# Gate and forget-logit projection of the forgetting branch: moved into the stick-breaking attention, one tile per step

## The reference

```
proj = h @ w_in
(q_r,k_r,v_r,g_r, q_s,k_s,v_s,g_s, q_f,k_f,v_f,g_f, f_logit) = split(proj)
o_r = group_norm(retention(rotary(q_r), rotary(k_r)/8, v_r))          # 6 heads of 64
o_s = stick_breaking(q_s, [cached k, k_s], [cached v, v_s])           # 5 heads
logf = log_sigmoid(f_logit + b_f);  C = cumsum(logf)                  # 5 heads
o_f = softmax(rms(q_f) . [cached k, rms(k_f)] / 8 + C_t - C_s) @ v    # 5 heads, causal
x = x + concat(o_r*silu(g_r), o_s*silu(g_s), o_f*silu(g_f)) @ w_out
x = x + (p @ w_pe) * sigmoid(rms_norm(x) @ w_pg)
```

## Time and profile before

| what | us |
|---|---|
| median of three runs | 3673.13 (3656.63 to 3677.41) |
| profiled execution: its own time | 3678.38 |
| profiled execution: span from first to last instruction | 3676.8 |
| TensorE, matmuls | 3204.2 busy (87%) |
| TensorE, weight loads | 1989.8 busy (54%) |
| VectorE | 1365.4 busy (37%) |
| ScalarE | 950.5 busy (26%) |
| GpSimd | 597.8 busy (16%) |
| mean granted TensorE clock | 0.929 of full |

### The profile page before, as it was taken

One profiled execution on the slowest core, in us unless ns is written; L12 is line 12 of the kernel. 1 busy time (PEld: TensorE's weight loads), 2 busy tenths in 40 slices (PEclk: granted clock), 3 DMA queues, 4 the chain that ended last, 5 costly groups with the idle time before them and its releaser, 6 DMA issues. The chain is left out here.

```text
span 3676.8 us, 67694 instructions
## 1 busy us (share of the span) xinstructions
PE 3204.2 (87%) x25256; PEld 1989.8 (54%) x25256; DVE 1365.4 (37%) x3002; ACT 950.5 (26%) x1746; POOL 597.8 (16%) x1090
## 2 busy tenths in 40 slices
PE   6999987888998688799989998978889987887998
PEld 4556654555666455444455666545556654554443
DVE  3235086443224444312142350954433244442211
ACT  2012144332224333211020122433322242331110
POOL 0000000444010044400000000004440101452000
PEclk9999988999999799899989999989999997998999
DMA  5011103887120388710120011048861205995102
GB/s 175 18 36 33 50 10 105 265 287 244 38 83 1 117 278 290 249 66 16 46 96 28 28 45 44 1 129 288 284 217 33 72 1 173 295 299 186 57 29 72
DMA packets 268657, 439.67 MB, mean 120 GB/s; under 512 B 48818, under 2 KB 216403, under 8 KB 268339
## 3 DMA queue, kind: packets, MB, share of 16 engines
q1 hardware_dynamic: 205810, 239.96, 20.4%
q0 software_dynamic: 55744, 189.25, 15.6%
q10 hardware_dynamic: 6912, 7.87, 0.6%
HBM read 410.28 MB, written 26.65 MB: 119 GB/s over the span
## 5 line engine op out<-in xcount | busy, mean ns | idle before, releaser
L806 PE MATMUL ps<-W,xT 128*128 128x320 f32 (+7 forms) x5120 | 1482.9, 465 | 11.5 <-DVEq L449 11.5
L806 PEld LDWEIGHTS ps<-W,xT 128*128 128x128 f32 (+1 forms) x5120 | 856.7, 184 | 585.6 <-issue 291.5
L688 POOL DMA_DIRECT2D branch<-in_cache_sb_v_dram x480 | 258.8, 539 | 637.5 <-issue 597.3
L688 POOL DMA_DIRECT2D branch<-in_cache_fox_v_dram x480 | 258.9, 539 | 621.2 <-issue 579.6
L1468 ACT ACTIVATE branch<-ps 128x512 f32<-128x512 f32 x288 | 165.6, 595 | 386.6 <-PE ps L1051 378.2
L1051 PE MATMUL ps<-C,W 128*128 128x128 f32 x1280 | 199.4, 301 | 73.1 <-DMA W<-in_cache_fox_k_dram 26.6
L1051 PE MATMUL ps<-C,branch 128*128 128x128 f32 x1280 | 194.9, 295 | 65.7 <-DMA branch<-in_cache_sb_k_dram 18.0
L1136 PE MATMUL ps<-branch 128*8 128x64 f32 x9920 | 182.2, 234 | 55.9 <-DMA branch<-in_cache_fox_v_dram 27.6
L1073 PE MATMUL ps<-branch,work 128*32 128x512 f32 x896 | 229.9, 631 | 0.8 <-issue 0.2
L1051 PEld LDWEIGHTS ps<-C,W 128*128 128x128 f32 x1280 | 151.0, 151 | 141.0 <-issue 67.4
L1051 PEld LDWEIGHTS ps<-C,branch 128*128 128x128 f32 x1280 | 147.8, 149 | 146.3 <-issue 96.1
(11 more groups left out here) (246 smaller groups left out, 3389.1 us busy)
## 6 DMA issues: line engine op xcount, KB each, us to landing
branch<-in_cache_sb_v_dram POOLq DMA_DIRECT2D x480, 160.0 KB, 4.3
branch<-in_cache_fox_v_dram POOLq DMA_DIRECT2D x480, 160.0 KB, 4.1
W<-in_cache_sb_k_dram SPq DMA_DIRECT2D x248, 160.0 KB, 3.4
W<-in_cache_fox_k_dram SPq DMA_DIRECT2D x248, 160.0 KB
branch<-in_cache_sb_k_dram SPq DMA_DIRECT2D x240, 160.0 KB, 4.2
branch<-in_cache_fox_k_dram SPq DMA_DIRECT2D x240, 160.0 KB, 4.3
W<-in_w_in_dram SPq DMA_DIRECT2D x14, 1280.0 KB, 6.3
W<-in_w_in_dram SPq DMA_DIRECT2D x9, 1536.0 KB, 7.1
```

The lines of the kernel that those rows point to most:

```text
L688: pool.dma_start(ringV[:, g % 2, p * DA:(p + 1) * DA], cache[L, bass.ds(pg, 1)].rearrange("a s h d -> s (a h d)"))\
L806: ins = pe.matmul(out, src[:, k, t * P:t * P + R], W[i % 2][:, k, a:z], start=(k == 0), stop=(k == kc - 1), **place)
```

## The change

The segment `fg` leaves `PROJ_F`. In `ATT_S` TensorE issues its nine tiles after the transposes of a unit: tile 0 at (i = 0, h = 1), tile k at (i = k - 1, h = 4). They all go to bank 7. The weighing has bank 6 alone, and the turn-back goes to bank 7, in both attentions. So the first weighing of a row tile waits for the copy of the one before (`att_copied`), and the turn-back waits for the `fg` tile to be emptied. ScalarE's and VectorE's shares of a tile stand between their units. The logits get a tensor of their own. The log forget values are made at the start of `fq`, the cumulative matmuls follow its last tile. `W[0]` now holds `fg`, `fq`, `fv` and `out0` in turn, `W[1]` holds `fk`. SP loads `fq` behind the ninth `fg` tile, `fk` after `DEC_S`, and `out0` after the last tile of `fv`.

```diff
@@ -60,6 +60,7 @@
 TURNED = {"rq": TILES, "rk": TILES, "sq": NT, "sk": NT, "fq": NT, "fk": NT}
+W_OF = {seg: (0 if seg in ("fq", "fv") else 1 if seg == "fk" else i % 2) for i, seg in enumerate(ALL_SEGS)}
 GATE_AT = {"rg": 0, "sg": DR, "fg": DR + DA}
@@ -87,7 +88,22 @@
     n = ALL_SEGS.index(seg) * TILES + t
-    return 3 + 4 * (n % 2) if seg in IN_RET else n % 3
+    return 3 + 4 * (n % 2) if seg in IN_RET else 7 if seg == "fg" else n % 3
+def same_buffer(seg):
+    return [s for s in ALL_SEGS[:ALL_SEGS.index(seg)] if W_OF[s] == W_OF[seg]]
+def loads_of(seg):
+    return 1 + sum(s != "rq" for s in same_buffer(seg))
+def att_fill_steps(k):
+    return (0, 1) if k == 0 else (k - 1, 4)
@@ -297,7 +313,7 @@
         squares = cut(work, 2200, HA, HD)
-        logit = cut(work, 2600, TILES, HA)
+        logit = sb("logit", [P, TILES, HA])[:]
         ltmp = cut(work, 2650, TILES, HA)
@@ -455,7 +471,7 @@
         PROJ_R, RET, PROJ_S, ATT_S, DEC_S, PROJ_F, ATT_F, DEC_F = range(8)
-        PROJ_SEGS = {PROJ_R: SEG_NAMES[0:4], PROJ_S: SEG_NAMES[6:8], PROJ_F: SEG_NAMES[8:12]}
+        PROJ_SEGS = {PROJ_R: SEG_NAMES[0:4], PROJ_S: SEG_NAMES[6:8], PROJ_F: SEG_NAMES[9:12]}
         OUT_SEGS, GATED_SEGS = ["out0", "out1"], ["pg0", "pe0", "pg1", "pe1"]
@@ -499,10 +515,10 @@
             def load_weights(L, seg):
-                i = ALL_SEGS.index(seg)
-                if i >= 2:
-                    sp.wait_ge(proj_ready, TILES * (i - 1))
+                users = same_buffer(seg)
+                if users:
+                    sp.wait_ge(proj_ready, TILES * (ALL_SEGS.index(users[-1]) + 1))
                 if seg in SEG_COL:
@@ -511,8 +527,8 @@
                     kc = PLE // P if seg[:2] == "pe" else KC
-                sp.dma_start(W[i % 2][:, 0:kc, 0:n], src.rearrange("(k p) n -> p k n", p=P))\
-                    .then_inc(w_loaded[i % 2], 16)
+                sp.dma_start(W[W_OF[seg]][:, 0:kc, 0:n], src.rearrange("(k p) n -> p k n", p=P))\
+                    .then_inc(w_loaded[W_OF[seg]], 16)
@@ -530,6 +546,8 @@
                 load_k(L, kind, 0, 0)
+                if kind == "sb":
+                    load_weights(L, "fq")
                 sp.wait_ge(phase_sem, 4 * ((ATT_S if kind == "sb" else ATT_F) + 1))
@@ -576,9 +594,9 @@
                 sp.wait_ge(phase_sem, 4 * (DEC_S + 1))
-                load_weights(L, "fq")
+                load_weights(L, "fk")
                 load_decoded(L, "sb")
-                for seg in ALL_SEGS[10:13]:
+                for seg in ALL_SEGS[11:13]:
                     load_weights(L, seg)
@@ -786,14 +804,14 @@
-                    pe.wait_ge(w_loaded[i % 2], 16 * ((i - 1) // 2 + 1))
+                    pe.wait_ge(w_loaded[W_OF[seg]], 16 * loads_of(seg))
                 if seg == "out0":
                     pe.wait_ge(norm_out, (TILES if seg == "pg0" else 0) + t + 1)
-                back = 2 if seg in IN_RET else 3
+                back = 2 if seg in IN_RET else 1 if seg == "fg" else 3
                 if n >= back:
@@ -803,7 +821,7 @@
                         place = dict(tile_position=(0, ROWS if a else 0), skip_group_check=True) if t == SAMPLE else {}
-                        ins = pe.matmul(out, src[:, k, t * P:t * P + R], W[i % 2][:, k, a:z],
+                        ins = pe.matmul(out, src[:, k, t * P:t * P + R], W[W_OF[seg]][:, k, a:z],
                                         start=(k == 0), stop=(k == kc - 1), **place)
@@ -841,7 +859,7 @@
                         turn_tile(seg, TILES - 1)
-                    if seg == "fg":
+                    if seg == "fq":
...
@@ -964,12 +982,13 @@
                     c = h // 2
-                    if c == 0 and i >= 2:
-                        pe.wait_ge(att_done[kind], i - 1)
+                    if c == 0 and i >= 1:
+                        pe.wait_ge(att_copied[kind], i)
                     heads = [(a, 2 * c + a) for a in range(2) if 2 * c + a < HA]
                         for a, hh in heads:
-                            ins = pe.matmul(ps[a * HD:(a + 1) * HD, 6 + t % 2, c * P:(c + 1) * P],
+                            ins = pe.matmul(ps[a * HD:(a + 1) * HD, 6, c * P:(c + 1) * P],
                                             v[:, j, hh * HD:(hh + 1) * HD],
@@ -978,10 +997,15 @@
-                    pe.wait_ge(att_copied[kind], NT - t)
+                    i = NT - 1 - t
+                    pe.wait_ge(att_copied[kind], i + 1)
+                    if i >= 1:
+                        pe.wait_ge(att_done[kind], i)
+                    if kind == "sb":
+                        pe.wait_ge(emptied_dve, evac_count("fg", i + 1))
                     for c in range(QP):
                         w = min(P, DA - c * P)
-                        ins = pe.transpose(ps[:, 6 + t % 2, c * P:c * P + w], att_oT[kind][0:w, c * P:(c + 1) * P],
+                        ins = pe.transpose(ps[:, 7, c * P:c * P + w], att_oT[kind][0:w, c * P:(c + 1) * P],
                                            ident[0:w, 0:w])
@@ -994,6 +1018,11 @@
                     turn(u)
+                    for k in range(TILES):
+                        if kind == "sb" and att_fill_steps(k) == (i, h):
+                            if i >= 1:
+                                pe.wait_ge(att_done[kind], i)
+                            segment_tile("fg", k, L)
                 weigh(len(UNITS) - 1)
...
@@ -1295,6 +1324,12 @@
                     i = ALL_SEGS.index(seg)
+                    if seg == "fq":
+                        act.wait_ge(logit_ready, 1)
+                        act.activation(ltmp, ltmp, ACT.Exp).then_inc(logf_act, 1)
+                        act.wait_ge(logf_act, 1)
+                        act.activation(ltmp, ltmp, ACT.Ln, bias=1.0).then_inc(logf_act, 1)
                     for t in range(TILES):
@@ -1360,12 +1395,6 @@
                         turned_to(seg, TILES - 1)
-                    if seg == "fg":
-                        act.wait_ge(logit_ready, 1)
-                        act.activation(ltmp, ltmp, ACT.Exp).then_inc(logf_act, 1)
-                        act.wait_ge(logf_act, 1)
-                        act.activation(ltmp, ltmp, ACT.Ln, bias=1.0).then_inc(logf_act, 1)
@@ -1428,8 +1457,8 @@
                         act.wait_ge(att_back[kind], NT - 1 - t)
-                    act.activation(att_oT[kind][:, 0:2 * P], ps[:, 6 + t % 2, 0:2 * P], ACT.Copy)
-                    act.activation(att_oT[kind][0:HD, 2 * P:3 * P], ps[0:HD, 6 + t % 2, 2 * P:3 * P], ACT.Copy)\
+                    act.activation(att_oT[kind][:, 0:2 * P], ps[:, 6, 0:2 * P], ACT.Copy)
+                    act.activation(att_oT[kind][0:HD, 2 * P:3 * P], ps[0:HD, 6, 2 * P:3 * P], ACT.Copy)\
                         .then_inc(att_copied[kind], 1)
@@ -1437,8 +1466,14 @@
                     to_sbuf(u)
+                    if kind == "sb" and h == 0 and i >= 1:
+                        gate_tile("fg", i)
+                    if kind == "sb" and (i, h) == (0, 2):
+                        gate_tile("fg", 0)
                     if h == 1 and i >= 1:
                         copy_out(t + 1)
+                if kind == "sb":
+                    gate_tile("fg", SAMPLE)
                 copy_out(0)
@@ -1598,9 +1633,9 @@
                     i = ALL_SEGS.index(seg)
-                    if seg == "fg":
-                        link(dve.memset(logit, 0.0))
+                    if seg == "fq":
                         link(dve.memset(logf_padded[:, 0:NT - 1], 0.0))
+                        dve.scalar_tensor_tensor(ltmp, logit, -1.0, logit, ALU.mult, ALU.min).then_inc(logit_ready, 1)
                     for t in range(TILES):
@@ -1696,12 +1731,12 @@
                             link(dve.tensor_tensor(out, out, gated[0:R, t % 2, :], ALU.add))
-                    if seg == "fg":
-                        dve.scalar_tensor_tensor(ltmp, logit, -1.0, logit, ALU.mult, ALU.min).then_inc(logit_ready, 1)
-                        dve.wait_ge(logf_act, 2)
-                        dve.scalar_tensor_tensor(logf, logit, 0.0, ltmp, ALU.min, ALU.subtract)\
-                            .then_inc(logf_ready, 1)
+                        if seg == "fq" and t == 2:
+                            dve.wait_ge(logf_act, 2)
+                            dve.scalar_tensor_tensor(logf, logit, 0.0, ltmp, ALU.min, ALU.subtract)\
+                                .then_inc(logf_ready, 1)
+                    if seg == "fq":
                         dve.wait_ge(cum_ready, 1)
@@ -1845,6 +1880,7 @@
                     link(dve.memset(prod[:, SEQ:SEQ + 1], 1.0))
+                    link(dve.memset(logit, 0.0))
@@ -1879,7 +1915,7 @@
                     out = O[:, t, at:at + DA]
-                    o = ps[:, 6 + t % 2, 0:DA]
+                    o = ps[:, 7, 0:DA]
                     if kind == "fox":
@@ -1888,10 +1924,16 @@
                     (stick if kind == "sb" else largest)(u)
+                    if kind == "sb" and h == 1 and i >= 1:
+                        gate_tile("fg", i)
```

(4 more changed lines are left out.)

## The result

The changed kernel took 3714.61 us (median of eight runs, 3694.23 to 3723.74) against 3681.84 for the kernel before on the same chips. The ratio is 1.0086 (95% interval 1.0060 to 1.0111): slower by about 32 us, where +0.15% was forecast and the range ended at 3701. The profiled execution took 3719.43 us with a span of 3717.9, so against the profiled execution before there are 41.1 us to explain.

The account below looks back on a forecast made before the run. VectorE was taken to bound the stick-breaking attention, with TensorE idling 4.04 us in the projection. Terms -87.8 + 85.7 + 5.9 + 1.6 = +5.4 on 3678.38 gave 3683.8; less 5.25 to the median, 3679 us (+0.15%), range 3657 to 3701.

Parts of the forecast that it names:

- VectorE sets the pace in the stick-breaking attention, and a tile stops it for its length less the slack: Stick-breaking attention, tiles 1 to 7: each 4.37 us tile stalls VectorE 4.29 us, as the slack averages 0.08.
- The gate adds 0.61 on VectorE: Stick-breaking attention: a tile's two VectorE instructions take 0.73 us, of which 0.12 fits idle time, so 0.61 more per tile.
- rival C: Stick-breaking attention: the weighing's wait shows there too, and the turn-back waits for the gate; 5.9 us more, 3685; chance 0.09.
- Tiles 0 and 8: Stick-breaking attention's start and end: tile 0 adds 5.1 and 5.0 us by layer, tile 8 adds 3.5 (2.3 to 4.6).
- The pause in the projection: Forgetting branch's projection: TensorE's idle 4.04 us goes, and the slow tiles behind it no longer lose 2.4 and 2.0 us.
- `out0`'s load: End of the projection: out0's 2 MB starts during the last value store the barrier awaits; 0.3 us per layer, bounds 0 and 4.
- Rival D: Decode and barrier: the moved loads delay them by their full length, 4 + 4 us per layer; 3694; chance 0.06.
- The other load that moved: Start of the stick-breaking decode: fq's late 1.3 MB load collides with the first pages; 0.5 us per layer, bounds 0 and 4.
- One bank for the weighing: Forgetting attention: first weighing waits 0.42 us for the copy at seven row-tile changes; 5.9 us in both layers, bounds 0 and 7.
- B: End of the stick-breaking attention: the clock falls to half earlier, 17 us per layer, 3713; chance 0.09.

Follow-up runs that it names:

- e4: The changed kernel with fg tile k issued after the transposes of unit h = 3 in place of h = 4; 3696.05 us, ratio 1.0033.
- e8: The changed kernel with the fg tiles cut to two of their eight matmuls over k; 3637.71 us (two executions), ratio 0.9872.
- e6: The kernel before, fg still first in the projection, its log forget values made during fq and cumulative matmuls after fq's last tile; 3663.20 us, ratio 0.9945.
- e3: The changed kernel with out0's weights loaded after the barrier that ends the forgetting branch's projection; 3697.66 us, ratio 1.0042.
- e1: The changed kernel with two banks and the old waits back in the forgetting attention; 3684.44 us, ratio 1.0016.
- e2: The kernel before with one bank for the weighing in the forgetting attention, which waits for the copy; 3699.98 us, ratio 1.0053.
- e5: The kernel of e2 with four unread transposes added after the unit's transposes at h = 4, 0 and 1 of the forgetting attention; 3686.76 us, ratio 1.0002.
- e7: The changed kernel with the edits of e1, e3 and e4 together; 3656.82 us, ratio 0.9928.

## Why the prediction was wrong

Its steps one by one:

- *VectorE sets the pace in the stick-breaking attention, and a tile stops it for its length less the slack.* Right. Forecast 4.29 us per tile, 4.16 to 4.38 measured wherever the clock was full (5.3 to 6.9 where it was at half), and e4 and e8 move it as the theory says, by the place and by the length.
- *The gate adds 0.61 on VectorE.* Right within about 0.3: VectorE starts the unit behind the gate 0.3 to 0.5 us later than the stall alone would have it. From the unit behind a gate to the next tile its delay against the kernel before doesn't grow where the clock is full (13.5 us all the way behind tile 2, 18.2 behind tile 3 in layer 0), so the weighing's wait costs nothing in this attention, as the prediction said; rival C did not come.
- *Tiles 0 and 8.* Tile 0 was put at 5.0 to 5.1 and cost 1.6 and 2.6 us by the mask of unit 4: the working let the clock rise at the same moment as before, and it rose at 20.1 and 20.5 us into the phase in place of 26.8 and 25.1. All twelve such phases with a tile 0, the quarter tile of e8 among them, have that rise at 20.1 to 21.9 us, the eight without at 25.0 to 27.4, so the tile brings it. Tile 8 was put at 3.5 and ran at half clock, its slower bound (4.67 us for the tile). With the clock's dips at tiles 2 and 5 in layer 0 and 2, 3 and 7 in layer 1, worth some 1 to 2.6 us each, the phase's sum was 88.9 against 85.7.
- *The pause in the projection.* Right: e6 alone gave 13.0 where the steps give 12. The projection shrank by 82.1 of the 87.8 forecast; without the 7.7 us that its barrier grew by it would be 89.8.
- *`out0`'s load.* Forecast 0.3 per layer, bounds 0 and 4; measured 3.4 and 4.3 between TensorE's end and the barrier. e3 shows that 5.7 of these 7.7 us are the load. Rival D named the place. The other load that moved is open: in layer 1 the stick-breaking decode grew by 7.7 us, where 0.5 was put for `fq`. It took 311.1 to 318.0 us in the four kernels that load `fq` late and 318.7 to 325.1 in the six that load it early; in layer 0 the same two groups overlap (319.0 to 321.0 and 315.6 to 325.0). No run moves this load alone, so the cause isn't shown.
- *One bank for the weighing.* This is the step that failed: "So it is on the path, at all seven changes of row tile: 2.9 us per layer, 5.9 in both, bounds 0 and 7." The wait itself was sized nearly right (0.51 for 0.42) and its place was right. What was missing is what it does to the granted clock: the step took TensorE's work behind the wait to last as long as before, and at half clock it didn't. The term was 29.5 us in place of 5.9. e1 takes it away and returns the kernel to 1.0016; e2 puts it alone into the kernel before and loses 0.53%.

All forgetting attentions of the profiled executions but e5's, layer 0 and layer 1:

| kernel | banks for the weighing | length, us | at half clock, us |
|---|---|---|---|
| before | two | 132.1, 129.7 | 31.8, 29.4 |
| e1 | two | 129.9, 129.5 | 29.7, 25.8 |
| e6 | two | 131.9, 132.1 | 31.6, 31.8 |
| e7 | two | 131.6, 132.2 | 34.8, 35.4 |
| changed | one | 146.8, 144.5 | 70.5, 61.3 |
| e2 | one | 148.3, 136.0 | 71.9, 39.1 |
| e3 | one | 140.4, 146.7 | 53.8, 70.4 |
| e4 | one | 150.0, 152.3 | 77.0, 86.1 |
| e8 | one | 136.0, 146.6 | 39.2, 70.2 |

The eight with two banks end at 132.2, the ten with one begin at 136.0. The lengthening is there whatever else was edited, and its size is not fixed.

The rival that told of the clock, B, looked for its fall in the stick-breaking attention, where the tiles fill TensorE, and didn't apply it to the phase in which a wait was added and no work. The earlier trace rows had a warning: the clock of the stick-breaking attention was at half at its start and at its end, and the forgetting attention of the kernel before was the same, at half until 16.1 us and from 125.3 us on in layer 0. A phase with such an end can lose more of its clock, and the sum had no term for that. The error of the chances was the same: 0.09 for the only rival in which the clock falls earlier, and nothing for a fall in the forgetting attention.

What stays open: the layer 1 decode above, why the clock falls at 98.2 us in one layer of e2 and at 118.2 in the other with the same program, and why e4's forgetting attention, unedited, was the worst of all. A phase near that edge seems to go one way or the other by where it stands when TensorE idles; that is argued, not shown.

## What to carry to other kernels

Work moved in one lump into a phase whose two engines take turns was hidden here only by the slack ahead of the very instruction it is put in front of: read that slack at the place (0.1 us at h = 4, about 1 us at h = 3), not the engine's idle share of the phase. When a change takes a buffer from somebody else to make room, price that other place too, and keep its rotation if nothing forces you to give it up: here it cost more than all the rest together. A wait added to a phase in which TensorE already idles now and then had two prices here, its own length and that of the half clock behind it; give the range the second one.

## What the runs showed of the hardware

More work can be faster, where it stands in TensorE's idle time: 88 added transposes that nobody reads took the forgetting attention of layer 0 from 148.3 to 142.9 us, with 35.9 in place of 71.9 us at half clock, and, with 88 more in layer 1, the kernel from 1.0053 to 1.0002. In layer 1, where little clock was lost, the same ones cost 3.3 us. The Trainium skill (TensorE: Matmul & The Clock Gate, HAM oscillation) tells of a matmul loop that falls back to the slow clock in each turn, while it waits for a DMA longer than it computes. This case agrees in the direction alone: here the clock fell with much shorter waits for ScalarE (1.5 to 1.7 us at a change of row tile), and the mean granted clock of that phase in layer 0 is 0.75 in e2 and 0.87 with e5's fillers. Over the eighteen forgetting attentions of the table the length goes with the time at half clock, from 129.5 us with 25.8 at half to 152.3 us with 86.1 at half: 22.8 us more of length for 60.3 more at half, some 0.4 for each.
